# Strassen's algorithm for the down projection of a two-layer decoder step, and norms with one token per partition

## What is computed

```
h = rms_norm(x, norm_mix_g);  z = h @ w_in          # columns shared by three mixers
x = x + (sum of gated mixer outputs) @ w_out
h = rms_norm(x, norm_ffn_g)
x = x + (silu(h @ w_ffn_gate) * (h @ w_ffn_up)) @ w_ffn_down
rms_norm(x, g) = x * rsqrt(mean(x * x over channels) + 1e-6) * g
```

## Time and profile before

| | |
|---|---|
| time, median of 3 runs (lowest to highest) | 3939.35 us (3935.71 to 3940.05) |
| time of the profiled execution | 3938.83 us |
| its span, first to last instruction | 3937.2 us |
| granted TensorE clock, mean | 0.945 of full |
| DVE, ACT, POOL busy | 36%, 19%, 7% |
| up and gate projections, layer 0 | 1543.7 to 1820.2 us |
| down projection, layer 0 | 1820.2 to 1974.8 us |

### The profile page before, as it was taken

One profiled execution on the slowest core, in us unless ns is written; L12 is line 12 of the kernel. 1 busy time (PEld: TensorE's weight loads), 2 busy tenths in 40 slices (PEclk: granted clock), 3 DMA queues, 4 the chain that ended last, 5 costly groups with the idle time before them and its releaser, 6 DMA issues. The chain is left out here.

```text
span 3937.2 us, 47054 instructions
## 1 busy us (share of the span) xinstructions
PE 3640.8 (92%) x18570; PEld 2840.1 (72%) x18570; DVE 1405.0 (36%) x3043; ACT 761.7 (19%) x1564; POOL 285.9 (7%) x396
## 2 busy tenths in 40 slices
PE   6899898989789999999988988989887899999999
PEld 5777765755558887888877677556555688878888
DVE  4714514557300013442055164235662000144411
ACT  2312323146200001000032132221551000010000
POOL 0000011024200000000000000110342000000000
PEclk9999988989889999999999998889898999999999
DMA  4111353120542221222122104522206321212121
GB/s 141 46 65 44 101 153 118 59 114 1 169 136 71 86 83 46 86 75 91 38 100 67 64 27 131 161 75 75 97 16 192 113 77 65 86 65 86 65 102 38
DMA packets 222171, 336.97 MB, mean 86 GB/s; under 512 B 56614, under 2 KB 122386, under 8 KB 217210
## 3 DMA queue, kind: packets, MB, share of 16 engines
q1 hardware_dynamic: 204474, 281.91, 22.1%
q0 software_dynamic: 8064, 43.00, 3.1%
q10 hardware_dynamic: 9408, 8.98, 0.7%
HBM read 313.50 MB, written 37.10 MB: 89 GB/s over the span
## 5 line engine op out<-in xcount | busy, mean ns | idle before, releaser
L368 PE MATMUL pair<-hT,ring 128*128 128x260 f32 (+1 forms) x3648 | 835.2, 390 | 48.3 <-PEq L1419 25.2
L368 PEld LDWEIGHTS pair<-hT,ring 128*128 128x128 f32 (+1 forms) x3648 | 699.6, 192 | 171.6 <-issue 56.7
L383 PE MATMUL pair<-ring,hT 128*128 128x512 f32 (+2 forms) x800 | 311.8, 556 | 5.5 <-PEq L1262 5.5
L2600 PE MATMUL pair<-arena,ring 128*128 128x260 f32 x1408 | 309.1, 383 | 2.7 <-DVE arena L2648 2.7
L2600 PEld LDWEIGHTS pair<-arena,ring 128*128 128x128 f32 x1408 | 267.4, 190 | 44.4 <-DVE arena L2648 3.4
L383 PEld LDWEIGHTS pair<-ring,hT 128*128 128x128 f32 (+1 forms) x800 | 151.8, 212 | 153.4 <-issue 152.8
L2564 DVE TENSOR_TENSOR arena<-pair,arena 128x520 f32<-128x520 f32 x48 | 33.6, 700 | 626.4 <-PE pair L368 626.4
L457 PE MATMUL pair<-obT,oaT 128*128 128x260 f32 x1056 | 246.3, 383 | 0.0
L457 PEld LDWEIGHTS pair<-obT,oaT 128*128 128x128 f32 x1056 | 201.3, 191 | 31.2
L2118 POOL TENSOR_SCALAR arena<-arena 128x128 f32<-128x128 f32 (+3 forms) x256 | 152.4, 611 | 506.5 <-DVE arena L2077 506.5
L457 PE MATMUL pair<-hT,ring 128*128 128x260 f32 x704 | 169.4, 395 | 17.2 <-DVE hT L583 17.2
(11 more groups left out here) (372 smaller groups left out, 4922.5 us busy)
## 6 DMA issues: line engine op xcount, KB each, us to landing
ring<-in_w_in_dram SPq DMA_DIRECT2D x38, 2048.0 KB, 8.6
ring<-in_w_ffn_gate_dram SPq DMA_DIRECT2D x10, 2048.0 KB, 7.8
ring<-in_w_ffn_up_dram SPq DMA_DIRECT2D x10, 2048.0 KB, 7.8
ring<-in_w_ffn_down_dram SPq DMA_DIRECT2D x8, 2048.0 KB, 7.6
out_s_win_kv_dram<-in_cache_win_kv_dram SPq DMA_DIRECT2D x2, 8176.0 KB
arena<-in_cache_slc_kv_dram SPq DMA_DIRECT2D x88, 128.0 KB, 3.0
ring<-in_cache_slc_kv_dram SPq DMA_DIRECT2D x84, 128.0 KB, 2.2
ring<-in_w_in_dram SPq DMA_DIRECT2D x64, 128.0 KB, 2.9
```

Of the source, the lines that this page charges most:

```text
L368: last = pe.matmul(pair[o][0:m, half, 0:HA], lhs(k), rhs[:, k, half * HA:(half + 1) * HA], start=(k == 0), stop=(k == nk - 1))
L383: last = pe.matmul(big[0:rows, 0:w], hT[:, k, tt * P:tt * P + rows], slab[:, k, 0:w], start=(k == 0), stop=(k == KT - 1))
L2600: last = pe.matmul(pair[m][:, half, 0:HA], w[:, k, m * P:(m + 1) * P], FA[:, r + k, half * HA:(half + 1) * HA], start=(r + k == 0), stop=( ...
```

## The change

**Down projection.** Twelve more steps (`DOWN_STEPS`): for each half of the outputs, each slab and each half of a slab, seven products of four matmuls (three for the slab with six row tiles). The result of a step is not collected in PSUM over the slabs but added at once to `xT` by eleven VectorE operations (`added_sums`), for which ScalarE copies `P1` out of its bank (`keep_first`). Each slab's part of `FA` gets its own four input sums (`input_sums` after `fu` steps 3, 7 and 10). TensorE waits at a down step for the `fu` products that its slab needs, not for the last one.

**Sums in place.** The seven sums of an up or gate step are written straight into their place in `GATE` or `FA` (`stored_sums`); SiLU runs once over both tiles, and the product with the gate is one operation of 1040 columns. The input sum `T1` overwrites the block `B12`, so `T3` is formed first. The weight sums move from `oaT` to the end of the arena.

**Norms.** VectorE adds the squares of the eight tiles (`add_square`, seven additions of 520 columns). Five matmuls with one column each (`norm_pe`) turn the sums so that each token has a partition; mean, root and reciprocal run on 4 columns of 128 partitions and 1 column of 8. Five matmuls of 128 columns (`spread_roots_pe`) spread the reciprocals over the partitions again, into banks 4 and 5, from which the last step (L583 before) reads them.

```diff
-    STEPS = [(n, i) for i in range(FT // 2) for n in ("fg", "fu")]
+    MERGE_STEPS = []
+    FFN_STEPS = [(n, i) for i in range(FT // 2) for n in ("fg", "fu")]
+    DOWN_STEPS = [("fd", hf, r, i) for hf in range(2) for r in range(0, FT, 8) for i in range(2)]
+    STEPS = MERGE_STEPS + FFN_STEPS + DOWN_STEPS
     ORDER = ("P1", "P2", "P5", "P6", "P3", "P7", "P4")
...
+    STORED = ("U2", "C11", "U5", "C12", "C22", "U3", "C21")
+    ADDED = ("X11", "U2", "C11", "U5", "C12", "X12", "C22", "U3", "X22", "X21", "C21")
...
+    def half_tiles(q):
+        return min(8, FT - STEPS[q][2]) // 2 if STEPS[q][0] == "fd" else 4
...
-        for k in range(4):
+        kh = half_tiles(q)
+        for k in range(kh):
             if made:
                 pe.wait_ge(*normed(made, "h", k + 1))
+            last = pe.matmul(step_bank(q, prod), a[:, k, :], b[:, k, :], start=(k == 0), stop=(k == kh - 1))
...
+    def input_sums(dve, name, inputs):
+        x, xsum = inputs[name]
+        n, done = 4 * SETS.index(name), sem("st_inputs")
+        dve.tensor_tensor(xsum["T3"], input_block(x, "B22"), input_block(x, "B12"), ALU.subtract).then_inc(done, 1)
+        dve.wait_ge(done, n + MADE_X["T3"])
+        dve.tensor_tensor(xsum["T1"], input_block(x, "B12"), input_block(x, "B11"), ALU.subtract).then_inc(done, 1)
+        dve.wait_ge(done, n + MADE_X["T1"])
+        dve.tensor_tensor(xsum["T2"], input_block(x, "B22"), xsum["T1"], ALU.subtract).then_inc(done, 1)
+        dve.wait_ge(done, n + MADE_X["T2"])
+        dve.tensor_tensor(xsum["T4"], xsum["T2"], input_block(x, "B21"), ALU.subtract).then_inc(done, 1)
+    def input_tiles(x, space):
+        kh = x.shape[1] // 2
+        return x, {"T1": input_block(x, "B12"), **{t: space.take(kh, HA) for t in ("T3", "T2", "T4")}}
...
+    def added_sums(dve, q, t, u1, u2, u5):
+        c_, done = quarters_of(t), sem("st_sums")
+        dve.wait_ge(sem("st_kept"), q + 1)
+        dve.tensor_tensor(c_["11"], c_["11"], u1, ALU.add).then_inc(done, 1)
+        add_product(dve, q, "U2", u2, u1, "P6")
+        add_product(dve, q, "C11", c_["11"], c_["11"], "P2", made="X11")
+        add_product(dve, q, "U5", u5, u2, "P5", made="U2")
+        add_product(dve, q, "C12", c_["12"], c_["12"], "P3", made="U5")
+        dve.wait_ge(*sums_done(q, "C12"))
+        dve.tensor_tensor(c_["12"], c_["12"], u5, ALU.add).then_inc(done, 1)
+        add_product(dve, q, "C22", c_["22"], c_["22"], "P7")
+        add_product(dve, q, "U3", u2, u2, "P7")
+        dve.wait_ge(*sums_done(q, "C22"))
+        dve.tensor_tensor(c_["22"], c_["22"], u5, ALU.add).then_inc(done, 1)
+        dve.wait_ge(*sums_done(q, "U3"))
+        dve.tensor_tensor(c_["21"], c_["21"], u2, ALU.add).then_inc(done, 1)
+        add_product(dve, q, "C21", c_["21"], c_["21"], "P4", ALU.subtract, made="X21")
...
+    def norm_pe(pe, tag, ms):
+        pe.wait_ge(*normed(tag, "sum", KT - 1))
+        for tt, n in TOKENS:
+            last = pe.matmul(bank[6][0:n, tt:tt + 1], ms[:, tt * P:tt * P + n], ones[:, 0:1], start=True, stop=True)
+        last.then_inc(sem("norm_sum"), 1)
+    def spread_roots_pe(pe, tag):
+        pe.wait_ge(*normed(tag, "ms", 2))
+        for tt, n in TOKENS:
+            last = pe.matmul(bank[4 + tt // NT][:, tt % NT * P:tt % NT * P + n], rstd[0:n, 1, tt:tt + 1].to_broadcast([n, P]),
+                             ident[0:n, 0:n], start=True, stop=True)
         last.then_inc(sem("norm_sum"), 1)
     def square_tile(act, tag, k):
         if k >= 2:
-            act.wait_ge(*normed(tag, "sum", k - 1))
+            act.wait_ge(*normed(tag, "sum", max(k - 2, 1)))
         act.activation(tag_sq[tag][k % 2], xT[:, k, :], ACT.Square).then_inc(sem("norm_sq"), 1)
-    def norm_root(act, tag, ms):
+    def add_square(dve, tag, k, ms):
+        dve.wait_ge(*normed(tag, "sq", k + 1))
+        if k >= 2:
+            dve.wait_ge(*normed(tag, "sum", k - 1))
+        dve.tensor_tensor(ms, tag_sq[tag][0] if k == 1 else ms, tag_sq[tag][k % 2], ALU.add
+                          ).then_inc(sem("norm_sum"), 1)
+    TOKENS = [(tt, P if tt < NT else NB) for tt in range(NT + 1)]
+    def token_columns(ap):
+        return ap[:, 0:NT], ap[0:NB, NT:NT + 1]
+    def norm_root(act, tag):
         act.wait_ge(*normed(tag, "ms", 1))
-        act.activation(ms, ms, ACT.Sqrt).then_inc(sem("norm_rt"), 1)
-    def norm_mean(dve, tag, ms):
+        for ap in token_columns(rstd[:, 0, :]):
+            last = act.activation(ap, ap, ACT.Sqrt)
+            if ap.shape[0] == P:
+                last.then_inc(sem("norm_rt"), 1)
+        last.then_inc(sem("norm_rt"), 1)
+    def norm_mean(dve, own, tag):
         dve.wait_ge(*normed(tag, "sum", KT))
-        dve.tensor_scalar(two(ms), both(2), 1.0 / DM, EPS, ALU.mult, ALU.add).then_inc(sem("norm_ms"), 1)
-    def norm_dve(dve, own, tag, ms, gain):
-        dve.wait_ge(*normed(tag, "rt", 1))
-        own(dve.reciprocal(ms, ms))
+        m, b = token_columns(rstd[:, 0, :]), token_columns(bank[6])
+        own.tick(dve.tensor_scalar(m[0], b[0], 1.0 / DM, EPS, ALU.mult, ALU.add))
+        own.wait()
+        dve.tensor_scalar(m[1], b[1], 1.0 / DM, EPS, ALU.mult, ALU.add).then_inc(sem("norm_ms"), 1)
+    def norm_dve(dve, own, tag, gain):
+        dve.wait_ge(*normed(tag, "rt", 2))
+        m, r = token_columns(rstd[:, 0, :]), token_columns(rstd[:, 1, :])
+        own(dve.reciprocal(r[0], m[0]))
+        dve.reciprocal(r[1], m[1]).then_inc(sem("norm_ms"), 1)
+        dve.wait_ge(*normed(tag, "sum", KT + 1))
+        both_banks = pair[2].rearrange("p a n -> p (a n)")[:, 0:TA]
         for k in range(KT):
-            dve.scalar_tensor_tensor(hT[:, k, :], xT[:, k, :], par[:, PR[gain] + k:PR[gain] + k + 1], ms,
+            dve.scalar_tensor_tensor(hT[:, k, :], xT[:, k, :], par[:, PR[gain] + k:PR[gain] + k + 1], both_banks,
                                      ALU.mult, ALU.mult).then_inc(sem("norm_h"), 1)
...
                     for m in range(4):
                         j = 4 * hf + m
                         proj_T(pe, ("wo", j), lambda k: w[:, k, m * P:(m + 1) * P], MG)
-                        if j:
-                            sum_tile(pe, "ffn", j - 1)
-                sum_tile(pe, "ffn", KT - 1)
+                norm_pe(pe, "ffn", ms8)
...
+                    if j >= 2:
+                        add_square(dve, "ffn", j - 1, ms8)
+                add_square(dve, "ffn", KT - 1, ms8)
...
+                spread_roots_pe(pe, "ffn")
+                for q in range(len(MERGE_STEPS), len(STEPS)):
+                    n, *k = STEPS[q]
                     open_slab(pe, step_slab(q))
-                    product(pe, q, "P1", wsum, hT, xsum, made="ffn" if q == 0 else None)
-                    if q == 0:
+                    if q == len(MERGE_STEPS):
+                        product(pe, q, "P1", wsum, inputs, made="ffn")
                         pe.wait_ge(*normed("ffn", "h", KT))
+                    else:
+                        if n == "fd":
+                            pe.wait_ge(sem("proj_read_dve"), dve_reads(("fu", min(k[1] // 2 + 4, FT // 2) - 1)))
+                        product(pe, q, "P1", wsum, inputs)
                     for prod in ORDER[1:]:
-                        product(pe, q, prod, wsum, hT, xsum)
-                pe.wait_ge(sem("proj_read_dve"), dve_reads(STEPS[-1]))
...
+                        product(pe, q, prod, wsum, inputs)
             @block.scalar
             def _(act):
-                norm_root(act, "ffn", ms8)
...
+                norm_root(act, "ffn")
+                for q in range(len(MERGE_STEPS), len(STEPS)):
+                    n, *k = STEPS[q]
                     if n == "fg":
...
-                        act.activation(GATE[:, 0, :], GATE[:, 0, :], ACT.Silu)
...
-                        act.activation(GATE[:, 1, :], GATE[:, 1, :], ACT.Silu).then_inc(sem("proj_read_act"), 1)
+                        if k[0]:
+                            act.wait_ge(sem("proj_read_dve"), dve_reads(("fu", k[0] - 1)))
+                        keep_first(act, q, GATE[:, 0, 0:HA])
+                        act.wait_ge(*sums_done(q, "C21"))
+                        act.activation(GATE, GATE, ACT.Silu).then_inc(sem("proj_read_act"), 1)
+                    elif n == "fu":
+                        keep_first(act, q, FA[:, 2 * k[0], 0:HA])
+                    else:
+                        act.wait_ge(*sums_done(q - 1, "U2" if q > NTH["fd", 0, 0, 0] else "C21"))
+                        keep_first(act, q, KEPT[0])
             @block.vector
             def _(dve):
                 own = Own(dve, sem("dve_own"), own_counts["dve"])
-                norm_mean(dve, "ffn", ms8)
-                weight_sums(dve, 0, wsum)
-                norm_dve(dve, own, "ffn", ms8, "ffn")
+                norm_mean(dve, own, "ffn")
+                weight_sums(dve, len(MERGE_STEPS), wsum)
+                norm_dve(dve, own, "ffn", "ffn")
                 dve.wait_ge(*normed("ffn", "h", KT))
-                input_sums(dve, hT, xsum)
```

(48 more changed lines are left out.)

139 lines of the change are left out of this document (54 added, 85 removed).

## The result

| | kernel before | changed kernel |
|---|---|---|
| time, median of 4 runs (lowest to highest) | 3938.4 us (3935.71 to 3940.05) | 3885.8 us (3881.93 to 3888.18) |
| profiled execution, its span | 3938.83, 3937.2 us | 3881.93, 3880.3 us |
| granted TensorE clock, mean | 0.945 | 0.949 |

The ratio is 0.9866, 95% interval 0.9849 to 0.9883: the changed kernel is 1.3% faster. The medians lie 52.6 us apart, the two profiled spans 56.9. The forecast was 50.3 us and 3889 us.

The account below looks back on a forecast made before the run. TensorE, busy 92% of the span, was taken as the bound, through its work and gaps. Terms -38.6 (down matmuls), -2.7 (seam), -9.6 (feed-forward norm) and +0.6 (mixer norm) gave -50.3 us: 3889 us, range 3879 to 3901.

Parts of the forecast that it names:

- Down matmuls and seam: Down projection: 308 matmuls for 352 save 19.3 us a layer; no wait for the last gate product saves 1.3.
- VectorE in the down steps: Down steps: VectorE's weight sums and eleven sums take 7.3 of 12.3 us or 6.8 of 9.2, costing nothing.
- the 2.4 us of cover: Short down steps: VectorE's 6.8 us of work in a step of 9.2 us leaves 2.4 us spare.
- the rival in which VectorE becomes the bound: Down steps: slower VectorE sums and unseen waits cost some 17 us, giving 3906 us; chance 0.04.
- Half clock in groups of three: Short down steps: rival that three-matmul groups run at half clock, adding 74 us, giving 3963 us; chance 0.02.
- Feed-forward norm: Norm ahead of the feed-forward part: 5.26 us of sum matmuls go, chain 0.5 later, clock 0.1 back: net 4.8 saved a layer.
- For the clock I took 0.1 us: Feed-forward norm: TensorE back at full clock sooner around P2, counted as 0.1 us gained of at most 1.1.
- a forecast of -9.0 for both norms: Both norms over both layers: feed-forward norm saves 9.6 us in all, mixer norm adds 0.6.
- Mixer norm: Norm ahead of the mixers: hT 0.4 us later, clock gives back 0.1: plus 0.3 us a layer, 0.6 in all.
- The lower bound: Low end from unknown costs: feed-forward norm saving 6.5 us and mixer norm -2.8 a layer, stated as 3880 us.
- Cheaper still: All four norms: rival that small matmuls restore full clock before hT, 9.6 us more saved, 3879 us; chance 0.06.

Follow-up runs that it names:

- late_inputs: Changed kernel with all three sets of the down projection's input sums moved behind the last up projection (last fu step); 3891.33 us.
- extra4: Changed kernel with four useless VectorE sums of 260 columns added in each down step; 3881.89 us, ratio 0.9868 to the kernel before.
- extra12: Changed kernel with twelve useless VectorE sums of 260 columns added in each down step; 3909.7 us, ratio 0.9943 to the kernel before.
- norms_only: Kernel before with the new norms alone, its down projection still the plain product; 3921.69 us, ratio 0.9965 to the kernel before.
- downs_only: Changed kernel with the old norms put back, keeping the new down projection and sums in place; 3891.86 us, ratio 0.9883 to the kernel before.
- warm: Changed kernel with useless TensorE matmuls ahead of and inside the norms' chains; 3874.57 us, ratio 0.9847 to the kernel before.

## Why the prediction was right

**Down matmuls and seam (-20.6 us a layer): right.** From the start of `P2` (1548.37, now 1538.66) to the end of layer 0 (1975.48, now 1944.90) it is 20.9 us less. The stage has the records, the duration of one and the clock that were forecast, and no idle row at its start; late_inputs shows what the early place of the input sums is worth there.

**VectorE in the down steps (nothing): right, and the 2.4 us of cover too, by two errors that cancel.** I counted weight sums of 384 columns in every short step, but the second one forms those of 512, 2.5 us for 2.1. The eleven sums take 4.2 to 4.3 us for 4.7: eight follow at 0.34 us and three at 0.46 to 0.52, about as forecast, but the 0.4 that I added at the end is covered by the next operation, which starts 0.34 us after the last sum starts. That leaves the 2.4 us of the trace there, and 3.15 in the first short step. extra4 and extra12 bracket the edge: the rival in which VectorE becomes the bound is a real mechanism, and this kernel stands on the near side of it.

**Half clock in groups of three: did not come.** The clock was granted at 1.00 over both down projections, with banks rotating and a third of the steps in groups of three. The section on psum-queue depth-cycling in the Trainium skill, "TensorE: Matmul & The Clock Gate", would have some of that time at the lower level; by the rows of this case none of it is. Where TensorE had stood for 2.3 us, in extra12, the six records behind the stall took 1.58 us at two places and 2.76 and 2.52 us at two others, for the same work. In late_inputs the clock fell behind a stall of 2.37 us in both layers. In these runs the full clock of the stage went with a TensorE that did not stand still.

**Feed-forward norm (-4.8 us a layer): right in sum, with the clock left open.** The period of `wo` is 7.01 us, and first to last addition is 5.26 us shorter, the figure of the forecast. The chain starts `hT` 0.0 and 0.5 us later, forecast 0.5; the spreading takes the slow value, 2.60 us. For the clock I took 0.1 us, of at most 1.1. From the first `hT` tile to the third product it was 9.14 us and is 9.10 in layer 0 and 8.11 in layer 1, so 0.0 and 1.0 came: one value stood for two outcomes, as the last section shows. norms_only, at -13.6 us against a forecast of -9.0 for both norms, had the full clock at `P2` in both layers: its third product starts 16.8 us after the last `wo` addition, for 18.6 in the kernel before.

**Mixer norm (+0.3 us a layer): the sign was wrong.** To the first `hT` tile I forecast 0.4 us more; it is 0.4 and 0.6 us less. The steps up to the last addition of squares came as forecast, at +7.33 us for +7.35. Then two terms were sized too high. The one-column matmuls took 2.0 us for 2.6, because I doubled the full-clock price and put the latency on top; at half clock they do not take twice the 1.18 us that they take at full clock. The nine turns took 1.4 us for 1.8. Together the spreading started at +11.9 instead of +12.9.

To the first copy the profiled pair gives -1.5 and -1.2 us. The part behind the `hT` tiles, -1.1 and -0.6, came with a full clock that was back earlier in the first projections: the earlier trace rows end at the `hT` tiles, and the windows from 5 to 10 us behind them, first of the kernel before and then of the changed one, are

```profile
2005.00:2010.00 5.00, 5.00 (x21) 4.24 (x20) 2.85 (x17) 0.00 (x0) 0.00 (x0) 0.86 0.50 182
```

```profile
1973.00:1978.00 5.00, 5.00 (x24) 4.35 (x23) 2.55 (x17) 0.00 (x0) 0.00 (x0) 1.00 0.74 271
```

That is 24 records for 21 in the same time. But this part is not shown to be the work of the change. From the first `hT` tile to the first copy the kernel before has 10.8 and 10.9 us and the changed one 9.7 and 10.3, yet five executions with the new norms unedited lie between 9.7 and 11.2, and downs_only, with the old norms, has 11.1 and 9.8. Of the -2.7 us, then, 1.0 are shown and the rest can be the scatter of the pair. With -1.0 us in place of +0.6 the sum of the forecast becomes -51.9 us, with -2.7 it becomes -53.6; the medians say -52.6 and -54.3. That an earlier clock comes from TensorE working a few microseconds before `hT` was only argued; warm, which puts more work there, changed the stretch from `hT` to the first copy by no more than its scatter.

**The lower bound** was added up wrongly: 3888.5 less 2 x 1.7 and 2 x 3.1 is 3879, the time of the rival *Cheaper still*, and not 3880. The median does not hang on it.

## What to carry to other kernels

Where the windows show a stage that is full at the full clock, a count of records times the duration of one forecasts it within a per cent, and the only question left is whether the other engines' queues fit under it: their slack stands in the waits of the unloaded trace, and adding junk to a queue until the time moves shows where it ends. A chain of small operations that crosses engines is mostly hand-overs and clock: doubling the full-clock price of small matmuls overstates it, and such a chain is best counted to the operation behind it at which TensorE is full again. The stretch behind such a chain scatters by more than 1 us from one execution to the next, so what a change does there is read from several. A part that gets faster pays only as far as what stands next in line does not wait for something else: of the 1.8 us that `P2` gained at full clock, 1.0 arrived. And a stall can cost more than its length, since the clock may fall behind it: 4.2 us for 2.4 in late_inputs.

## What the runs showed of the hardware

The same code ran at either clock level in one execution. In layer 1 of the changed kernel the one-column matmuls and `P2` are

```profile
3449.26 1.18 PE L624 MATMUL pair<-con,arena 128*128 128x1 f32 x10 [2.20 <-DVE arena L645]
...
3462.07 2.02 PE L477 MATMUL pair<-hT,ring 128*128 128x260 f32 x8 [0.81 <-DVE hT L676]
3464.71 1.99 PE L477 MATMUL pair<-hT,arena 128*128 128x260 f32 x8 [0.62 <-DVE hT L500]
```

and in layer 0 they took 1.68 and 3.84 us, behind the same chain and nearly the same idle times. The windows over `P2`, layer 0 and layer 1, have the two levels:

```profile
1538.66:1542.50 3.84, 3.84 (x9) 3.08 (x10) 3.74 (x4) 0.96 (x1) 0.00 (x0) 0.50 0.00 0
3462.07:3464.09 2.02, 2.02 (x8) 1.44 (x8) 1.99 (x2) 0.91 (x1) 0.00 (x0) 1.00 0.00 0
```

Where `P2` runs at the full level, the next wait is for an input sum (L500), so only 1.0 of its 1.8 us arrive. The third product starts 17.6 us after the last `wo` addition for 19.1; the other 0.5 is the faster one-column matmuls, with which `hT` starts at 9.5 instead of 10.0. Five executions were read that have these norms with no edit in them (the changed kernel twice, late_inputs, extra4 and extra12); each had one layer near 17.6 and the other at 18.7 or 19.1. norms_only, whose input sums have the old order, had `P2` at the full level in both. What decides it was not found. The ten records of the one-column matmuls took 1.18 us at a granted clock of 1.00, 1.99 at 0.50 and 1.68 at a mean of 0.61, so a factor of 1.7 and not of 2 lies between the levels.
